# Two blocks on one core: products of weights and values with the values stationary, and head norms with features on partitions

## What is computed

```python
h = rmsnorm(x, attn_norm_w);  proj = h @ w_in
y_sb = from_heads(stick_breaking_attention(q_a, k_a, v_a))       # 4 heads
y_ch = from_heads(chunked_relpos_attention(qh, kh, v_b, bias))   # 8 heads: probs @ v, probs = softmax
y_cv = short_conv_mixer(g_b, g_c, x_c, conv_w)                   # 256 channels
y = group_rmsnorm(concatenate([y_sb, y_ch, y_cv]), out_norm_w)   # mean over each group of 64
x = x + y @ w_out
x = x + swiglu(rmsnorm(x, ffn_norm_w), w_gate, w_up, w_down)
```

## Time and profile before

| | before |
|---|---|
| median of 3 runs | 693.56 us |
| the profiled execution's own time | 693.62 us |
| its span in the profile | 691.9 us |
| mean granted TensorE clock | 0.997 |
| PE busy | 684.5 us (99%), 3814 instructions |
| PE weight loads | 589.4 us (85%) |
| DVE busy | 485.4 us (70%), 739 instructions |
| ACT busy | 413.8 us (60%), 701 instructions |
| POOL busy | 93.8 us (14%), 163 instructions |
| DMA | 126.14 MB, 182 GB/s |

### The profile page before, as it was taken

One profiled execution on the slowest core, in us unless ns is written; L12 is line 12 of the kernel. 1 busy time (PEld: TensorE's weight loads), 2 busy tenths in 40 slices (PEclk: granted clock), 3 DMA queues, 4 the chain that ended last, 5 costly groups with the idle time before them and its releaser, 6 DMA issues.

```text
span 691.9 us, 9481 instructions
## 1 busy us (share of the span) xinstructions
PE 684.5 (99%) x3814; PEld 589.4 (85%) x3814; DVE 485.4 (70%) x739; ACT 413.8 (60%) x701; POOL 93.8 (14%) x163
## 2 busy tenths in 40 slices
PE   9999999999999999999999999999999999999996
PEld 8888888888888888888888888888888888888885
DVE  6878697768666666667465767777768877777774
ACT  7786764656555555546555866555567665555553
POOL 2023021688100000002710000000000000000001
PEclk9999999999999999999999999999999999999998
DMA  9936533746555555536434335554454555455401
GB/s 343 389 124 234 193 122 129 267 160 232 193 183 185 194 195 205 195 123 218 182 129 172 122 122 190 185 197 176 170 207 155 206 216 187 182 183 187 180 0 62
DMA packets 19484, 126.14 MB, mean 182 GB/s; under 512 B 2416, under 2 KB 2544, under 8 KB 5232
## 3 DMA queue, kind: packets, MB, share of 16 engines
q1 hardware_dynamic: 19296, 125.34, 49.9%
q10 hardware_dynamic: 144, 0.20, 0.1%
HBM read 124.48 MB, written 1.05 MB: 181 GB/s over the span
## 4 chain that ended last, share of the span: by engine, by line
PE 94%; DVE 2%; DMA 1%; ACT 1%; SPq 1%; issue 0%; POOL 0%; POOLq 0%
PE bank L222 91%; PE bank L231 3%; DMA raw<-in_w_dram 1%; DVE wlo L243 1%; SPq L511 1%; ACT whi L234 0%; DVE xsq L243 0%; DVE sc L1282 0%; DVE xres L243 0%; ACT L234 0%; ACT sc L234 0%; DVE qa L247 0%; POOL rstd L243 0%; POOLq L1522 0%; DVE last L243 0%
## 5 line engine op out<-in xcount | busy, mean ns | idle before, releaser
L243 DVE TENSOR_TENSOR wlo<-raw,whi 128x1024 fp32r<-128x1024 f32 x222 | 271.3, 1234 | 62.7 <-ACT whi L234 59.6
L234 ACT ACTIVATE whi<-raw 128x1024 fp32r<-128x1024 f32 x222 | 230.7, 1052 | 4.8 <-PE bank L222 3.8
L222 PE MATMUL bank<-xb,whi 128*128 128x512 f32 x496 | 124.3, 392 | 0.1
L222 PE MATMUL bank<-xa,whi 128*128 128x512 f32 x432 | 108.3, 393 | 0.0
L222 PEld LDWEIGHTS bank<-xb,whi 128*128 128x128 f32 x496 | 90.4, 188 | 17.7 <-ACT zv L234 0.4
L222 PE MATMUL bank<-whi,xb 128*128 128x512 f32 (+1 forms) x352 | 96.2, 355 | 0.0
L222 PEld LDWEIGHTS bank<-xa,whi 128*128 128x128 f32 x432 | 78.9, 188 | 15.7
L222 PEld LDWEIGHTS bank<-xb,wlo 128*128 128x128 f32 x496 | 67.6, 190 | 4.9
L222 PEld LDWEIGHTS bank<-whi,xb 128*128 128x128 f32 x352 | 62.1, 189 | 9.4 <-ACT vtok L234 0.3
L222 PE MATMUL bank<-xb,wlo 128*128 128x256 f32 x496 | 69.1, 282 | 0.0
L222 PEld LDWEIGHTS bank<-xa,wlo 128*128 128x128 f32 x432 | 58.9, 190 | 4.2
(11 more groups left out here) (244 smaller groups left out, 935.2 us busy)
## 6 DMA issues: line engine op xcount, KB each, us to landing
raw<-in_w_dram SPq DMA_DIRECT2D x109, 1024.0 KB, 4.8
first<-in_first_dram SPq DMA_DIRECT2D x8, 388.0 KB, 6.2
raw<-in_w_dram SPq DMA_DIRECT2D x4, 512.0 KB, 8.9
bias<-in_bias_dram SPq DMA_DIRECT2D x1, 1024.0 KB, 8.7
xres<-in_x_dram SPq DMA_DIRECT2D x1, 1024.0 KB, 8.4
gain<-in_ffn_norm_w_dram SPq DMA_DIRECT2D x1, 512.0 KB, 9.2
gain<-in_mix_norm_g_dram SPq DMA_DIRECT2D x1, 512.0 KB, 9.9
gain<-in_ffn_norm_g_dram SPq DMA_DIRECT2D x1, 512.0 KB, 5.0
```

The source lines that it names most:

```text
L222: return P(lambda e: e.matmul(o, l, r, start=start, stop=stop), *w, inc=inc)
L234: return A(lambda e: e.activation(o, i, f, **kw), *w)
L243: return q(lambda e: e.tensor_tensor(out=o, in0=a, in1=b, op=op), *w)
```

## The change

- **Values stationary.** `sb_out` and `ch_out` now take a pair of heads. The stationary operand is 64 columns of values, the moving one the weights of a head (256 columns for the first 128 keys, 128 for the others), and the two heads of a pair write to partitions 0 to 63 and 64 to 127 of a bank: the result has features on partitions.
- **Softmax.** The division by the sum moves ahead of the transposes: `ch_norm`, run by `later` after each pair of scores, is a reciprocal and four scalar products on DVE. `ch_probs` transposes blocks in another order.
- **Finish.** Now `squares` (ACT Square, ACT copy to fp32r, DVE low part), `sums` (two products of 512 columns with a block matrix of ones: the sums over each 64 features, on every partition), `scaled` (ACT Ln with EPS as bias, ACT Exp with scale -0.5, two DVE `scalar_tensor_tensor` with gain and root), `split` (ACT copy, DVE low part). No transposes, no POOL, and the convolution's output needs none either.
- **Order.** Weights are transposed one unit later after their scores than before; `ch_out(6)` and the finish of group 1 move into the loop over k.
- **Set-up.** POOL writes the block matrix (`blk`, in the place of a work tile, then `blk_r`) and a constant; `parts_sq` lies on qa and on qta with kta, which are dead by then.

```diff
+    memset(blk[:, :], 0.0)
+    memset(blk[0:64, 0:64], 1.0, (G.sem, G.count))
+    g = memset(blk[64:128, 64:128], 1.0)
+    blk_tok = G(lambda e: e.tensor_copy(blk_r[:, :], blk[:, :]), g)
+    eps_tok = memset(eps[:, :], EPS)
...
-    def sb_out(h):
-        gm = wk[4 * (h % 2) + 3]
-        c = slice(h * 64, h * 64 + 64)
-        o0, o1 = pb[7][:, h * 64:h * 64 + 64], pb[7][:, 256 + h * 64:256 + h * 64 + 64]
-        mm(o0, gm[:, 0:128], va[:, 0, c], True, True, sb["w", h], *sb["v"], *bank_free[7])
-        mm(o1, gm[:, 128:256], va[:, 0, c], True, False)
-        sb["out", h] = [mm(o1, gm[:, 256:384], va[:, 1, c], False, True, inc=True)]
+    def sb_out(b):
+        for k in range(2):
+            for i in range(2):
+                h, gm = 2 * b + i, wk[4 * i + 3]
+                o = pb[7][64 * i:64 * i + 64, 256 * b + 128 * k:256 * b + 256]
+                mm(o, va[:, k, h * 64:h * 64 + 64], gm[:, 256 * k:256 + 128 * k], k == 0, k == 1,
+                   sb["w", h], *sb["v"], *bank_free[7])
+        sb["out", 2 * b] = sb["out", 2 * b + 1] = [P.mark()]
     finishes = [0]
-    sq_free, ytok = {0: [], 1: []}, {}
-    def finish(bank, kt, ptok, den_col=None, den_tok=None):
+    set_free, ytok = {0: [], 1: []}, {}
+    def finish(y, ybank, kt, ytoks, sbank):
         n = finishes[0]
         finishes[0] += 1
...
+        f, (h, l), z = sq[n % 2], parts_sq[n % 2], yt[n % 2]
+        parts, summed = [], []
+        def squares():
+            a = act(f[:, :], y, ACT.Square, *ytoks, *set_free[n % 2], *sq_free[n % 2], scale=0.125)
+            parts.append(copy(h[:, :], f[:, :], a))
+            parts.append(low(l[:, :], f[:, :], h[:, :], parts[0]))
+        def sums():
+            P.wait(*parts, blk_tok, *bank_free[sbank])
+            mm(pb[sbank][:, :], blk_r[:, :], h[:, :], True, False)
+            mm(pb[sbank][:, :], blk_r[:, :], l[:, :], False, True)
+            summed.append(P.mark())
         def scaled():
-            v.append(tt(V, by64(y[:, :]), by64(src), over64(r8), ALU.mult, *g, stok))
-        def transposed():
-            P.wait(*v)
+            a = act(f[:, :], pb[sbank][:, :], ACT.Ln, *summed, eps_tok, bias=eps[:, 0:1])
+            bank_free[sbank] = [a]
+            a = act(f[:, :], f[:, :], ACT.Exp, a, scale=-0.5)
+            v = []
             for b in range(2):
...
+                c = slice(b * 256, b * 256 + 256)
+                v.append(stt(z[:, c], y[:, c], vec[:, V_ON + kt + b:V_ON + kt + b + 1], f[:, c], ALU.mult, ALU.mult,
+                             a, *ytoks))
+            if ybank is not None:
+                bank_free[ybank] = v
+            return v
+        def split(v):
+            src, o = z[:, :].rearrange("p (k t) -> p k t", k=2), xb_h[:, kt:kt + 2, :]
+            a = copy(o, src, *v)
+            ytok[kt] = ytok[kt + 1] = low(xb_l[:, kt:kt + 2, :], src, o, a)
+            set_free[n % 2] = [a, ytok[kt]]
+        return squares, sums, scaled, split
...
+    def ch_scores(h):
+        ch_score(h)
+        ch_score(h + 1)
+        later(lambda: ch_norm(h))
+    def ch_norm(h):
+        g, r = h // 4, h % 4
+        pair = [x[:, :].rearrange("p (g t h) -> p g t h", g=2, t=2)[:, g, :, r:r + 2] for x in (rden, den)]
+        v = reciprocal(*pair, ch["e", h], ch["e", h + 1])
+        for i in range(2):
+            s = wk[r + i]
+            for c, t in ((slice(0, 256), 1), (slice(256, 384), 0)):
+                one = rden[:, g * 8 + t * 4 + r + i:g * 8 + t * 4 + r + i + 1]
+                ch["e", h + i] = ts(V, s[:, c], s[:, c], one, None, ALU.mult, None, v)
     def ch_probs(h):
+        ch_prob(h)
+        ch_prob(h + 1)
+    def ch_prob(h):
         bank, s, pt = 6 + h % 2, wk[h % 4], wk[4 + h % 4]
         used_before = ch["out", h - 4] if h >= 4 else sb["out", 2] + sb["out", 3]
         P.wait(ch["e", h], *bank_free[bank])
-        for i in range(3):
-            tr(pb[bank][:, i * 128:i * 128 + 128], s[:, i * 128:i * 128 + 128])
+        for c, i in enumerate((2, 0, 1)):
+            tr(pb[bank][:, c * 128:c * 128 + 128], s[:, i * 128:i * 128 + 128])
         p = P.mark()
         ch["T", h] = [p]
         ch["pT", h] = copy(pt[:, :], pb[bank][:, 0:384], p, *used_before)
         bank_free[bank] = [ch["pT", h]]
     def ch_out(h):
...
-    def ch_finish(g):
...
+        bank, c0 = 2 + h // 4, 256 * (h // 2 % 2)
+        for k in range(2):
+            for i in range(2):
+                v, pt = vb[:, k, (h + i) * 64:(h + i) * 64 + 64], wk[4 + (h + i) % 4]
+                mm(pb[bank][64 * i:64 * i + 64, c0 + 128 * k:c0 + 256], v, pt[:, 256 * k:256 + 128 * k], k == 0, k == 1,
+                   ch["pT", h + i], *ch["v"], *bank_free[bank])
+        ch["out", h] = ch["out", h + 1] = [P.mark()]
...
             sb_out(0)
-            sb_out(1)
             sb_scores(1)
             later(lambda: sb_parts(1))
         elif n == 2:
             sb_after(1)
             k_roots()
         elif n == 1:
-            sb_out(2)
-            sb_out(3)
-            sb_roots, sb_scaled, sb_finish = finish(7, 0, sb["out", 3][0])
-            sb_roots()
+            sb_out(1)
+            sb_squares, sb_sums, sb_scaled, sb_split = finish(pb[7][:, :], 7, 0, sb["out", 3], 6)
+            sb_squares()
             ch_transposes(qb, qtb, qn, "qT")
         elif n == 2:
             kn = k_scaled()
         else:
-            sb_scaled()
+            sb_sums()
             ch_transposes(kb, ktb, kn, "kT")
+    later(lambda: later(lambda v=sb_scaled(): sb_split(v)))
...
     conv_unit(0)
-    sb_finish()
-    ch_score(0)
-    ch_score(1)
+    ch_scores(0)
     conv_unit(1)
-    ch_probs(0)
-    ch_probs(1)
-    ch_score(2)
-    ch_score(3)
+    ch_scores(2)
     conv_taps(0)
     conv_unit(2)
+    ch_probs(0)
+    ch_scores(4)
+    conv_unit(3)
     ch_out(0)
-    ch_out(1)
     ch_probs(2)
-    ch_probs(3)
-    ch_score(4)
-    ch_score(5)
-    conv_unit(3)
-    ch_out(2)
-    ch_out(3)
-    ch_roots, ch_scaled_0, ch_finish_0 = ch_finish(0)
-    later(ch_roots)
-    ch_probs(4)
-    ch_probs(5)
-    ch_score(6)
-    ch_score(7)
+    ch_scores(6)
     conv_taps(1)
     conv_unit(4)
+    ch_out(2)
+    squares_0, sums_0, scaled_0, split_0 = finish(pb[2][:, :], 2, 2, ch["out", 2], 0)
+    squares_0()
+    ch_probs(4)
+    conv_unit(5)
     ch_out(4)
-    ch_out(5)
     ch_probs(6)
-    ch_probs(7)
-    conv_unit(5)
-    ch_scaled_0()
-    ch_out(6)
-    ch_out(7)
-    ch_roots, ch_scaled_1, ch_finish_1 = ch_finish(1)
-    later(ch_roots)
+    sums_0()
+    later(lambda: split_0(scaled_0()))
...
+    cv_squares, cv_sums, cv_scaled, cv_split = finish(flat(cvy[:, :, :]), None, 6, [cv["out"]], 1)
+    later(cv_squares)
     for k in range(KT - HOLD):
         u, lh, ll, w = mix_1(k)
         out_unit(u, (0, 1), lh, ll, k == 0, False, *w)
         release(u)
         if k == 0:
-            ch_finish_0()
...
+            ch_out(6)
+            squares_1, sums_1, scaled_1, split_1 = finish(pb[3][:, :], 3, 4, ch["out", 6], 0)
+            squares_1()
         elif k == 1:
-            ch_scaled_1()
-        elif k == 2:
-            ch_finish_1()
-            cv_scaled()
-        elif k == 3:
-            cv_finish()
+            sums_1()
+            cv_sums()
+            later(lambda: later(lambda v=scaled_1(): split_1(v)))
+            later(lambda: later(lambda v=cv_scaled(): cv_split(v)))
```

More of the change, by code:

```diff
@@ L524, in two_block_program @@
     N = Arena(phase)
+    qa_at = N.lo
     qa = N("qa", [128, 2, 512])
@@ L531, in two_block_program @@
     vb = N("vb", [128, 2, 512])
+    qta_at = N.lo
     qta = N("qta", [128, 2, 256])
@@ L546, in two_block_program @@
     L_h, L_l = [[at(wk_at + (4 * i + j) * 1536, f"L{j}{i}", [128, 384], F32R) for i in range(2)] for j in range(2)]
+    blk = at(wk_at + 1024, "blk", [128, 128])
     dgr_h, dgr_l = [at(N.lo + 1024 * i, f"dgr{p}", [128, 256], F32R) for i, p in enumerate("hl")]
@@ L549, in two_block_program @@
     sq = [N(f"sq{i}", [128, 512]) for i in range(2)]
-    st = N("st", [128, 4, 16])
+    blk_r = N("blk_r", [128, 128], F32R)
+    eps = N("eps", [128, 1])
+    parts_sq = [[at(o + 2048 * j, f"sq{p}{o}", [128, 512], F32R) for j, p in enumerate("hl")] for o in (qa_at, qta_at)]
     hst = N("hst", [128, 2, 2, 16])
@@ L724, in finish @@
-        return roots, scaled, transposed
-    ch = {}
+                c = slice(b * 256, b * 256 + 256)
[9 more added lines that the diff above has]
+            set_free[n % 2] = [a, ytok[kt]]
@@ L729, in head_norm @@
+        return squares, sums, scaled, split
+    ch, sq_free = {}, {0: [], 1: []}
     def head_norm(x, toks, n):
@@ L788, in ch_out @@
     def ch_out(h):
[L789 to L793, removed]
-    def ch_finish(g):
-        v = V(lambda e: e.reciprocal(rden[:, g * 8:g * 8 + 8], den[:, g * 8:g * 8 + 8]), ch["e", 4 * g + 3])
-        return finish(2 + g, 2 + 2 * g, ch["out", 4 * g + 3][0], 8 * g, v)
+        bank, c0 = 2 + h // 4, 256 * (h // 2 % 2)
[5 more added lines that the diff above has]
```

(17 more changed lines are left out.)

## The result

The changed kernel takes 695.81 us (median of 7 runs, 695.24 to 696.21), the kernel before 693.77 in the same comparison: ratio 1.0031, 95% interval 1.0021 to 1.0041, so it is slower by 2.0 us. The forecast was 695.3.

What follows compares the result with a forecast made beforehand. PE bounds the kernel now; after the change a ring of DVE and ACT makes it wait: -2.6 us of PE's work plus 4.4 of waits gives +1.8, so 695.3 us, range 691.0 to 697.2 (main case 694.9 to 696.6).

Steps and rivals of the forecast that it cites:

- a ring of DVE and ACT: Scores, DVE reductions, ACT exponentials, weight splits and join wait for each other; turns become 6.5, 6.4 and 5.9 us; chance 0.50.
- PE's own work: Products -2.0, transposes -2.2, sums by the block matrix +1.8, wait at conv_unit(0) -0.2: together -2.6 us if PE never waits.
- The waits: Six places where PE waits for DVE or ACT, together 4.4 us, with ends of 0 and about 6.2.
- sb_out(1): Step 1: the second head's weights end at 57.73 and its products now come at once; wait 0.2 us.
- scores(4): Step 2: PE is there at 77.0, the second bank is read out at 77.4; late by 0.3 us.
- scores(6): Step 3: PE is there at 82.8, banks free at 83.3 and 83.8; late by 1.0 us.
- ch_out(4): Step 4, the largest: ACT copies the transposed weights of heads 4 and 5 only after squares_0; late by 1.9 us.
- sums_0: Step 5: DVE's low part of the squares comes at 96.1, PE is there at 95.7; late by 0.5 us.
- sums_1: Step 6: PE is there at 103.1, the low part comes near 103.7 after ACT's other work; late by 0.5 us.
- Rival D: Pairs of heads: the halves of 256 columns don't run side by side, 3.8 us more, about 697.5; chance 0.03.
- Rival E: PE's clock in this stage: eight matmuls at half clock after a wait cost 1.8 us more, 697.1; chance 0.02.
- rival C: PE stays the bound, 691.0 up to 692.1, if heads 4 and 5's weights are copied by 92.1 for ch_out(4); chance 0.18.

Runs made afterwards that it cites:

- e1_no_norm: The changed kernel without ch_norm, so the softmax weights of the chunked heads are not divided by their sums: 691.98 us, ratio 0.9975 to the kernel before.
- e2_copies_first: The changed kernel with squares_0 queued behind ch_probs(4), so ACT copies the transposed weights of heads 4 and 5 first: 695.67 us, ratio 1.0031 to the kernel before.
- e4_norm_pool: The changed kernel with the four scalar products of ch_norm on POOL, the reciprocal still on DVE: 695.63 us, ratio 1.0029 to the kernel before.
- e7_moves: The changed kernel, ch_norm as it is, with transposes of qb ahead of sb_out(1) and cv_sums ahead of sums_1: 695.61 us, ratio 1.0028 to the kernel before.

## Why the prediction was right

The mechanism was the forecast one: PE has less to do, and a ring of DVE and ACT makes it wait at the places named. The time came out within 0.5 us in part by luck, since both terms of the sum were too small and they have opposite signs. The stage is measured from PE's last matmul ahead of the first products (42.78 before, 42.84 now) to the transposes of the next norm (117.91 before, 120.20 now): it is 2.2 us longer.

**PE's own work.** Summed at -2.6, it was -2.9: the same stage of e1_no_norm (42.27 to 115.84) is 1.6 us shorter than before's, with 1.4 us of waits in it. A pair of heads costs 0.80 to the next start and 0.14 in its neighbours (0.09 before it, 0.05 in the transposes behind), 0.94 for the 0.98 of the sum. The transposes were as said; the sums are 0.23 each, and 0.08 more where they stand behind transposes (91.95 to 92.26 in e1_no_norm, where nothing waits). The wait at conv_unit(0) went, and so did one of 0.1 at the first transposes of weights, which I had not counted.

**The waits.** Summed at 4.4, measured 5.1, by the steps of the prediction: sb_out(1) 0.46 (said 0.2), scores(4) 0.36 (0.3), scores(6) 0.45 + 0.54 = 1.0 (1.0), ch_out(4) 1.9 (1.9), sums_0 0.7 (0.5), sums_1 0.7 (0.5). The starts of the reductions were off by 0.2 to 0.3. The largest miss is at sb_out(1), where the second head waits for ACT:

```profile
56.59 0.99 ACT L234 ACTIVATE wk<-wk 128x384 f32<-128x384 f32 x2 [1.76 <-DVE wk L243]
```

The products start at 57.17 and the second head's weights are there at 57.58. I had left both on the clock of the kernel before; from the start of the stage PE gets there 0.45 us sooner, since the first pair is shorter, and the weights come only 0.2 sooner. At sums_0 the low part of the squares is ready at 96.35 for the 96.1 of the sum. At sums_1 the matmul behind the wait takes 0.07 more as well (104.14 to 104.44 is 0.30, not 0.23).

**The weighing of the page.** The Trainium skill (TensorEngine Tiling (Array Packing), Theoretical Speedup) gives up to twofold where a dimension is at most 64. The prediction worked 3.9 us out from that, all products halved. Measured is 0.94 for 1.28, so 0.34 five times, and 0.48 for the first, 2.2 in all; that is within the "up to", a factor of 1.36. The same page of the Trainium skill (Key Properties) says that a change of tiling mode drains TensorE. The trace agrees: 0.09 us on the way in. Rival D falls: the eight passes take 0.80 us to the next start, where it wanted over 1.2, so the halves run side by side. Rival E, the clock: the granted clock is 1.00 from 68 to 98 and from 98 to 112 us; a wait of 1.5 us in this stage did not lower it.

**What I had wrong in the reading.** I called ch_out(4) the place where the case is decided. It is the largest wait, but putting it right alone gave nothing (e2_copies_first); the ring's own speed decides, which the prediction's first paragraph had said and its rivals then left. Of rival C the sum was about right (-2.6 for -2.9) and its point wrong: in e2_copies_first ch_out(4) starts 1.2 us sooner, and nothing is gained. It takes a faster ring, not an earlier copy. Rival C also counts on DVE's idle time in each turn; the turns with taps have none.

## What to carry to other kernels

When work is moved off the bounding engine, follow the engines that feed it round their loop, not their busy share: DVE was at 70% of the span (25.0 of the 30 us from 68 to 98) and had 2.1 us idle in two of the three turns, yet each 0.93 us put on it came out at the end in full. New work in such a loop belongs where the engine waits for the other anyway; that alone was worth 1.9 us here. In a turn that the engine fills by itself no place helps, only less work. And before mending the longest wait, work out when the next one would end: a wait that is a symptom comes back under another name.

A scale per token and head ahead of a norm over that head's 64 features cancels but for the EPS; leaving it out gave the most of all the steps here, 3.8 us, and whether the EPS can be spared is for the owner of the model to say.

## What the runs showed of the hardware

- POOL's scalar product over 256 and 128 columns of f32 took 0.8 us on average (3.12 for four) and 1.15 in the turn at 90.91 (e4_norm_pool), against 0.25 on DVE (1.01 for four).
- Two f32 products with 64 stationary columns each, in the two column halves, run side by side at 256 moving columns too: eight passes in 0.80 us.
- A wait of PE costs its length and some 0.1 us more in the matmul behind it: 0.30 to the next start for 0.23 at 104.14, 0.34 for 0.23 at 110.49 in e7_moves.
- TensorE's granted clock stayed at 1.00 over the wait of 1.5 us at 93.93.
- The place of the whole timeline shifts by up to 1 us between profiles of nearly the same kernel, from the start on (the first product of weights and values at 42.6 to 43.6 us), so differences within a trace say more than its span.
